# Where the output projection of a recurrent layer crosses from one block of instructions into the next: three tiles finished before the seam, one at once behind it

## The reference: what is computed

```
# layer 0, per head (8 heads of 128)
o = gla_chunked(q, k, v, log_f, s0, chunk)          # gated linear recurrence
o = rms_norm(o, norm_g) * silu(gate)
out = einsum('bte,ed->btd', o, w_out)               # 1152 x 1024 times 1024 x 1024
x = layer_norm(ALPHA * x + out, ln_g, ln_b)
# layer 1 starts with two projections of x
kv = einsum('btd,de->bte', x, w_dkv)
proj = einsum('btd,de->bte', x, w_in_b)             # 2560 columns
```

## Time and profile before

| | |
|---|---|
| median of 3 runs | 1989.67 us (1986.71 to 1990.49) |
| the profiled execution, own time | 1989.84 us |
| its span, first to last instruction | 1987.9 us |
| TensorE busy | 97% of the span, granted clock 0.989 in the mean |
| VectorE, ScalarE, GpSimd busy | 54%, 39%, 21% |
| last turn of block A, from the end of the last projection | 534.3 us |
| first matmul of block M | 579.3 us |
| first matmul behind the first two column tiles | 714.3 us |

### The profile page before, as it was taken

How to read it: one execution, slowest core, us unless ns; L and a number is a source line. 1 busy time by engine, 2 the same in 40 slices (tenths; PEclk the granted TensorE clock), 3 DMA queues, 4 the chain that set the end, 5 groups by cost and what they waited for, 6 DMA issues and landing times.

```text
span 1987.9 us, 31444 instructions
## 1 busy us (share of the span) xinstructions
PE 1927.6 (97%) x11755; PEld 1818.5 (91%) x11755; DVE 1071.4 (54%) x1941; ACT 768.5 (39%) x1343; POOL 408.2 (21%) x333
## 2 busy tenths in 40 slices
PE   8999999999969999999999999999999989999998
PEld 8999999999957899999989999999999979988886
DVE  4355545554747611332266666667666567753532
ACT  4333233323311131221265565555555457761100
POOL 0222132213322110000032432433433410000000
PEclk9999999999989999999999999999999999999999
DMA  5122022202344311224212112011111252363421
GB/s 173 40 75 67 21 66 76 65 22 67 114 148 141 102 46 57 75 78 129 89 38 66 34 53 64 28 50 47 53 47 41 68 135 68 94 243 133 153 85 43
DMA packets 189459, 158.82 MB, mean 80 GB/s; under 512 B 36192, under 2 KB 173920, under 8 KB 189120
## 3 DMA queue, kind: packets, MB, share of 16 engines
q1 hardware_dynamic: 183584, 137.31, 23.1%
q10 hardware_dynamic: 5328, 18.88, 2.6%
q0 software_dynamic: 464, 1.48, 0.2%
HBM read 115.78 MB, written 41.84 MB: 79 GB/s over the span
## 4 chain that ended last, share of the span: by engine, by line
PE 53%; DVE 8%; issue 5%; ACT 3%; DMA 1%; POOL 0%; DVEq 0%; ACTq 0%; SPq 0%; POOLq 0%
PE ps L115 16%; PE ps L117 16%; PE ps L116 15%; PE ps L1846 1%; PE ps L1829 1%; PE ps L1828 1%; DVE h_pt_l L109 1%; ACT h_p L1962 1%; ACT h_p L1951 1%; DVE h_p L2050 1%; DVE h_mx L2088 1%; DVE h_p L2045 1%; DVE s_mx L2689 1%; PE ps L2356 0%; DMA m_x<-in_x 0%
## 5 line engine op out<-in xcount | busy, mean ns | idle before, releaser
L1742 POOL TENSOR_SCALAR h_p<-h_p,h_rsum 128x128 f32<-128x128 f32 (+7 forms) x128 | 220.7, 1726 | 443.1 <-DVE h_rsum L2092 443.1
L115 PE MATMUL ps<-act_h,a_w_l 128*128 128x384 f32 x768 | 270.8, 353 | 1.7 <-DVE act_l L109 1.7
L117 PE MATMUL ps<-act_h,a_w_h 128*128 128x384 f32 x768 | 260.1, 339 | 0.0
L116 PE MATMUL ps<-act_l,a_w_h 128*128 128x384 f32 x768 | 259.9, 338 | 0.0
L115 PE MATMUL ps<-act_h,m_c_l 128*128 128x384 f32 x480 | 163.7, 341 | 4.2 <-DVE act_l L109 2.4
L116 PE MATMUL ps<-act_l,m_c_h 128*128 128x384 f32 x480 | 163.2, 340 | 0.0
L117 PE MATMUL ps<-act_h,m_c_h 128*128 128x384 f32 x480 | 163.1, 340 | 0.0
L115 PEld LDWEIGHTS ps<-act_h,a_w_l 128*128 128x128 f32 x768 | 144.2, 188 | 6.4 <-issue 3.3
L116 PEld LDWEIGHTS ps<-act_l,a_w_h 128*128 128x128 f32 x768 | 144.3, 188 | 3.3 <-issue 3.3
L117 PEld LDWEIGHTS ps<-act_h,a_w_h 128*128 128x128 f32 x768 | 144.1, 188 | 0.0
L104 ACT ACTIVATE h_pt_h<-ps 128x128 fp32r<-128x128 f32 (+2 forms) x192 | 87.0, 489 | 112.0 <-PE ps L1846 111.8
(11 more groups left out here) (321 smaller groups left out, 4863.5 us busy)
## 6 DMA issues: line engine op xcount, KB each, us to landing
a_w_raw<-in_w_in_a SPq DMA_DIRECT2D x32, 512.0 KB, 4.1
m_c_raw<-in_w_in_b SPq DMA_DIRECT2D x20, 512.0 KB, 4.2
scratch_gate<-m_sg SPq DMA_DIRECT2D x16, 576.0 KB, 5.2
o_w_raw<-in_w_out_b SPq DMA_DIRECT2D x16, 512.0 KB, 6.8
h_gate<-scratch_gate SPq DMA_DIRECT2D x62, 128.0 KB, 2.1
scratch_og<-h_gate SPq DMA_DIRECT2D x62, 128.0 KB, 1.7
o_g_raw<-scratch_og SPq DMA_DIRECT2D x24, 256.0 KB, 4.1
a_xn<-in_x SPq DMA_DIRECT2D x9, 512.0 KB, 4.3
```

The lines of the kernel that those rows point to most:

```text
L115: nc.tensor.matmul(out, ll, rh, start=first, stop=False)
L116: nc.tensor.matmul(out, lh, rl, start=False, stop=False)
L117: return nc.tensor.matmul(out, lh, rh, start=False, stop=last)
L1742: nc.gpsimd.tensor_scalar(weights_of(u), weights_of(u), rsum[:, u % PB], None, ALU.mult).then_inc(S["p_ready"], 1)
```

## The change

It redraws which part of the projection belongs to which block, and reorders the streams of block M to match.

* Block A: rows 0 to 7 of tiles 0, 1 and 2 (24 pairs). Row 6 of tiles 0 and 1 stands after step 15; all of tile 2 and row 7 of all three tiles stand behind the last step, `SOT`. The g buffers are now two pairs of tiles, (0,1) and (2,3), the second where `a_qq` to `a_kdec` were. Heads 0 to 6 of tiles 2 and 3 are loaded by one new transfer (896 KB). Row 7, the last head, is rounded straight from `a_sg`. `low_row(4)` and what follows it stand one place earlier on VectorE.
* Block M: TensorE starts with the product of tile 3, for which everything has been rounded in block A. Tile t is turned three products later than it is multiplied (two and two at the end) instead of one later. Its `sum_done` waits follow the new banks (`py`, `pt`).
* x(0) is the first transfer of SyncE's queue and x(1) the third; `load_x` serves tiles 2 to 8. The attention output comes in pairs of tiles. `kvw_raw` is loaded when the product of tile 7 is done (`y_done` 8), before when that of tile 2 was. `gain` and `shift` are the first transfers of GpSimd.
* `norm`: (x - mean) * gain and x * deviation + shift, each as two instructions of 512 columns on VectorE, in place of five instructions on VectorE and GpSimd.

```diff
 BESIDE_STEPS = {1: [(0, 1)], 3: [(0, 0)], 5: [(1, 1), (1, 0)], 7: [(2, 1), (2, 0)], 9: [(3, 1), (3, 0)],
-                11: [(4, 1), (4, 0)], 13: [(5, 1)], 15: [(5, 0)]}
+                11: [(4, 1), (4, 0)], 13: [(5, 1), (5, 0)], 15: [(6, 1), (6, 0)],
+                16: [(0, 2), (1, 2), (2, 2), (3, 2), (4, 2), (5, 2), (6, 2), (7, 0), (7, 1), (7, 2)]}
+
+OUT_PARTS = [(0, slice(0, EARLY), slice(0, 2)), (0, slice(EARLY, EARLY + 1), slice(0, 2)), (2, slice(0, EARLY + 1), slice(0, 1)),
+             (0, slice(KD - 1, KD), slice(0, 2)), (2, slice(KD - 1, KD), slice(0, 2)), (2, slice(0, EARLY + 1), slice(1, 2))]
...
+                    sp.wait_ge(operand[3], AH)
+                    sp.wait_ge(pe_did["SI"], AH)
+                    sp.wait_ge(pe_did["K1"], AH)
+                    sp.wait_ge(og_stored, 16 * (EARLY + 1))
+                    sp.dma_start(sh.g2_raw[:, 0:EARLY + 1].rearrange("p h a t -> p h (a t)"),
+                                 d["scratch_o"][0:EARLY + 1, :, 2 * P:4 * P].rearrange("h p t -> p h t")).then_inc(o_loaded[2], 16)
...
                     if not proj:
                         high_row(6)
+                        high_o(1)
+                        high_o(2)
                     copy_o("SO", 2, h)
                 if not proj:
                     high_row(7)
-                    high_o(1, slice(EARLY, EARLY + 1))
+                    high_o(3)
+                    high_o(4)
+                    high_o(5)
...
                     scores(1)
                     states(1)
+                    if not proj:
+                        low_row(4)
                     gated("OT0", 0)
...
+    def py(t):
+        b = (4, 0, 2, 6)[t] if t < 4 else (0, 2)[t % 2]
+        return bank[:, b:b + 2]
...
+        sp.dma_start(x[:, 0], row("x", 0)).then_inc(x_loaded[0], 16)
+        load_pair(4)
+        sp.dma_start(x[:, 1], row("x", 1)).then_inc(x_loaded[1], 16)
+        load_columns(0)
+        load_columns(1)
...
+        sp.wait_ge(y_done, 4)
+        load_pair(6)
+        sp.wait_ge(y_done, 5)
+        load_pair(8)
+        sp.wait_ge(y_done, 8)
+        sp.dma_start(kvw_raw[:], d["w_dkv"].rearrange("(a p) e -> p a e", p=P)).then_inc(kv_loaded, 16)
...
+        pe.sem_inc(y_done, 3)
+        for t in range(3, NT):
+            if t > 3:
+                pe.wait_ge(gl_ready, t - 3)
+                pe.wait_ge(sum_done, t - 2 if t < 6 else t - 1)
             for kt in range(nk):
...
+                last = rows_product(nc, py(t), sh, kt, t)
             last.then_inc(y_done, 1)
-            if t == 2:
-                turn_tile(0, 0, False)
-            turn_tile(t - 1, (t - 1) % 2, t >= 3)
+            if t < 7:
+                turn_tile(t - 3)
+            elif t == 7:
+                turn_tile(4)
+                turn_tile(5)
+            else:
+                turn_tile(6)
+                turn_tile(7)
...
+        pe.wait_ge(cl_ready, 2)
+        pe.wait_ge(sum_done, 8)
+        pe.wait_ge(tl_done, 4)
+        columns(1, 0)
+        pe.wait_ge(sum_done, 9)
+        columns(0, 0)
+        turn_tile(NT - 1)
+        pe.wait_ge(tl_done, 7)
+        columns(0, 1)
+        pe.wait_ge(tl_done, 9)
+        columns(1, 1)
...
+        for t in range(NT):
+            finish(t)
+            if t + 2 < NT:
+                load_x(t + 2)
+            if t < 3:
+                high_g(t + 6)
...
             for c in halves:
-                nc.vector.tensor_tensor(x[:, par, c], x[:, par, c], gain[:, c], ALU.mult).then_inc(gain_done, 1)
...
+                nc.vector.scalar_tensor_tensor(out=x[:, par, c], in0=x[:, par, c], scalar=mv[:, 0:1], in1=gain[:, c], op0=ALU.subtract, op1=ALU.mult).then_inc(gain_done, 1)
+
+            dve.wait_ge(rstd_step, t * 2 + 2)
+            for h, c in enumerate(halves):
+                dve.wait_ge(gain_done, t * 2 + 1 + h)
+                nc.vector.scalar_tensor_tensor(out=x[:, par, c], in0=x[:, par, c], scalar=rstd[:, 0:1], in1=shift[:, c], op0=ALU.mult, op1=ALU.add).then_inc(x_ready, 1)
```

More of the change, by code:

```diff
@@ L850, in body @@
                 if not proj:
-                    low_row(4)
+                    low_row(5)
                 if gla:
                     square(1)
+                    normed(1)
                     if not proj:
-                        low_row(5)
-                    normed(1)
+                        low_row(6)
+                        low_o(1)
                     sample_states(0)
@@ L860, in body @@
                     if not proj:
-                        low_row(6)
+                        low_o(2)
                     normed(2)
@@ L941, in middle_programs @@
     sh = k.shared
[L942 removed]
+    w_h, w_l = sh.w_h, sh.w_l
     cq_at = kept_at + 4 * 4 * T
@@ L1107, in _ @@
     def _(pool):
+        pool.dma_start(gain[:], ln_g.partition_broadcast(P)).then_inc(ln_loaded, 16)
+        pool.dma_start(shift[:], ln_b.partition_broadcast(P)).then_inc(ln_loaded, 16)
         nc.gpsimd.memset(mhalf[:], -0.5).then_inc(const_set, 1)
@@ L1191, in columns @@
                 mm.then_inc(c_done, 1)
-        for i in range(2):
-            pe.wait_ge(cl_ready, i + 1)
-            pe.wait_ge(sum_done, NT - 1 + i)
-            for tg in range(NTG - 1):
-                pe.wait_ge(tl_done, 4 + 3 * tg)
-                columns(i, tg)
-        turn_tile(NT - 1, (NT - 1) % 2, True)
+        pe.wait_ge(cl_ready, 2)
[9 more added lines that the diff above has]
+        columns(1, 1)
         pe.wait_ge(tl_done, NT + 1)
@@ L1402, in norm @@
             nc.vector.bn_aggr(mv[:], flat(stats[:])).then_inc(mv_done, 1)
-            dve.wait_ge(rstd_step, t * 2 + 2)
-            nc.vector.tensor_scalar(x[:, par], x[:, par], mv[:, 0:1], rstd[:, 0:1], ALU.subtract, ALU.mult).then_inc(norm_done, 1)
-            if isinstance(t, int) and t == 0:
+            if t == 0:
                 dve.wait_ge(ln_loaded, 32)
-            dve.wait_ge(norm_done, t + 1)
+            dve.wait_ge(mv_done, t + 1)
             halves = [slice(0, BANK), slice(BANK, D)]
             for c in halves:
-                nc.vector.tensor_tensor(x[:, par, c], x[:, par, c], gain[:, c], ALU.mult).then_inc(gain_done, 1)
-            dve.wait_ge(gain_done, t * 2 + 2)
-            nc.vector.tensor_tensor(x[:, par, halves[1]], x[:, par, halves[1]], shift[:, halves[1]], ALU.add).then_inc(x_ready, 1)
-        norm(0, 0)
-        norm(1, 1)
+                nc.vector.scalar_tensor_tensor(out=x[:, par, c], in0=x[:, par, c], scalar=mv[:, 0:1], in1=gain[:, c], op0=ALU.subtract, op1=ALU.mult).then_inc(gain_done, 1)
[3 more added lines that the diff above has]
+                nc.vector.scalar_tensor_tensor(out=x[:, par, c], in0=x[:, par, c], scalar=rstd[:, 0:1], in1=shift[:, c], op0=ALU.mult, op1=ALU.add).then_inc(x_ready, 1)
+        norm(0)
+        low_g(4)
+        norm(1)
+        turned_low(0)
+        low_g(5)
+        norm(2)
+        turned_low(1)
+        norm(3)
+        low_g(6)
         low_columns(0)
+        turned_low(2)
+        norm(4)
+        low_g(7)
         low_columns(1)
-        low_g(3)
-        turned_low(0, 0)
-        turned_low(1, 1)
-        for t in range(4, NT):
-            norm(t - 2, t % 2)
-            low_g(t)
-            turned_low(t - 2, t % 2)
-        norm(NT - 2, (NT - 2) % 2)
-        turned_low(NT - 2, (NT - 2) % 2)
-        norm(NT - 1, (NT - 1) % 2)
-        turned_low(NT - 1, (NT - 1) % 2)
+        turned_low(3)
+        norm(5)
+        low_g(8)
+        norm(6)
+        turned_low(4)
+        turned_low(5)
+        norm(7)
+        turned_low(6)
+        norm(8)
+        turned_low(7)
+        turned_low(8)
         dve.wait_ge(kvh_ready, 1)
```

176 lines of the change are left out of this document (76 added, 100 removed).

## The result

The changed kernel takes 2001.57 us in the median (1996.02 to 2002.21, five runs) against 1989.67 us before (1986.71 to 1991.50, five runs on the same chip); the ratio is 1.0051, 95% interval 1.0034 to 1.0069. That is slower by 7 to 14 us. The prediction was 1990.7 us with a range up to 1999, so the median lies 2.6 us above its end. The execution whose trace is read here took 1996.02 us; it is the fastest of the five. A second set of five executions on another chip gave 1997.29 against 1990.70 us, ratio 1.0037 [1.0023, 1.0051]; that median lies inside the range.

A forecast was written before the change was run, and what follows sets the result against it. TensorE, busy for 97% of the span, was taken to bound the kernel. Losses of 30.2 us afterwards against 29.3 before made it 0.9 us slower than the profiled 1989.84 us: 1990.7 us, range 1981 to 1999 us (8 in 10).

The forecast's parts named there:

- what block A loses: Block A up to `SOT`: the chain of VectorE and GpSimd to `SOT` was left 0.4 us of new loss.
- the clock behind the waits: Block M: TensorE at 1.2 GHz costs 0.8 us behind product 4's wait, 5.1 us behind those of products 6 to 8.
- Products 6, 7 and 8: Block M: each product waits for a sum whose x is loaded behind a turn; 5.9, 5.9 and 6.8 us, 18.6 together.
- `SOT` before 571: End of block A, a sign to look for in the profile after: `SOT` runs before 571 us, forecast at 569.7.
- The seam: Barrier from block A to block M: the last store's 7.46 us wait is covered, 1.9 us of idle stays.
- the seam gives nothing: Rival at the barrier: it takes 7.5 us whatever stands ahead, 5.6 us of gain fail, 1996 us; chance 0.04.
- Start of block M: Product 4 waits for norm(0), `low_g(4)` and norm(1)'s sum, starting at 14.3 instead of 11.8 us: 2.5 us lost.
- The rule of the Trainium skill on the clock: Waits for transfers always drop TensorE's clock: the three new waits would, block A's exit would cost none; sum unchanged.
- Lost before: Kernel before, 556 to 714 us: TensorE loses 20.4 us idle and 8.9 us by the clock, together 29.3 us.
- The end: End of block M: the 2.37 us wait goes; `columns(0, 0)` waits 0.9 us for norm(8)'s sum instead.
- Transfers collide at every wait: Rival on the x loads: landings of 6.5 us lengthen the waits by 9 us, 2000 us; chance 0.17.
- The three new waits are hidden: Rival at products 6 to 8: x arrives in time, 18.6 and 5.1 us are not lost, 1967 us; chance 0.10.

The follow-up runs named there:

- Three turns: Changed kernel with tiles 2, 3 and 4 transposed in the middle of products 5, 6 and 7 instead of behind them: 1980.03 us, ratio to before 0.9939.
- The stores of x: Changed kernel with finished x tiles stored by SyncE as soon as ready, not by ScalarE behind the next load: 1995.77 us, ratio to before 1.0032.
- Row 0: Changed kernel with row 0 of tile 0 waiting only for `g_out` and of tile 1 only for `v_out`: 1995.32 us, ratio to before 1.0026.
- The 1280 KB load: Changed kernel with `kvw_raw` loaded when the product of tile 8 is done, instead of tile 7: 2001.07 us, ratio to before 1.0056.

## Why the prediction was wrong

The three waits ahead of products 6 to 8 were there, as forecast in place and size. What failed are two terms of the sum: what block A loses, put at 0.4 us and measured 2.56, and the clock behind the waits, put at 5.9 us in all and measured 7.8. In the seam the sum came out too low by 4.3 us (185.25 less 180.03 less 0.9); against the other two traces of before it is 5.8 us. The median missed by 10.9 us (2001.57 against 1990.7), so the seam explains less than half of that; the rest stays open, as said at the end of this section. By its own steps:

* **Products 6, 7 and 8: right.** Forecast 5.9, 5.9 and 6.8 us, measured 5.92, 5.96 and 7.34: +0.6. *Three turns* shows the cause. Two errors inside nearly cancelled: the load is issued 0.9 us sooner than I took, and 512 KB land in 4.3 and 4.4 us, not 3.8, since a store runs beside them (*The stores of x*). That the size came out so close is in part luck. The landing of x(6), put at 5.5 us, took 6.6, beside 7.3 for `kvw_raw`, in the list of DMA issues by window:

```profile
m_x<-in_x ACTq DMA_DIRECT2D x1, 512.0 KB, 4.4
...
m_kvw_raw<-in_w_dkv SPq DMA_DIRECT2D x1, 1280.0 KB, 7.3
...
m_x<-in_x ACTq DMA_DIRECT2D x1, 512.0 KB, 6.6
```

* **What block A loses: the step that failed.** "I leave 0.4 us." It lost 2.56, because row 0 of tile 1 now stands behind `g_out`, which VectorE signals with the gating instruction `a_sg` (L845) at 538.21 + 1.34 us. I had followed the new banks of tile 2 and the steps around `SOT`, and passed over the two lines of the change that make row 0 of every tile wait for `g_out` and for `v_out`. *Row 0* shows the cause and the price. Without it `SOT` would have run some 2.6 us before its 573.64. The sign "`SOT` before 571" failed with it. Of the rest, the wait at row 4 went, and `SOT` came without idle. The 896 KB took 7.6 us (7 estimated); ScalarE waited 2.87 us for them, TensorE did not.
* **The seam: right.** 1.9 forecast, 1.60 measured; nothing of the last store's 7.46 us is left. The rival "the seam gives nothing" is refuted.
* **Start of block M: right.** 2.5 forecast, 0.71 + 1.26 = 1.97 measured in idle; product 4 starts 14.2 us behind the first matmul, 14.3 forecast, and VectorE got `shift` at 9.0 us, as taken. The clock behind it was put at 0.8; it was 1.5 in this trace and 0 in the second.
* **The clock behind the waits: the second step that failed, by its size.** Forecast 5.1, measured 1.4 + 2.0 + 2.9 = 6.3, and with the start of block M 7.8 against 5.9. The longest wait, 7.34 us, was followed by the longest stretch, 6.13 us; I had given all three the mean of two stretches of 4.0 and 4.8 us.
* **The rule of the Trainium skill on the clock.** The three long waits all dropped the clock, in both traces of the changed kernel, so with that section ("HAM oscillation", page "TensorE: Matmul & The Clock Gate") the trace agrees. It also agrees at the exit of block A, where the clock stayed at 1.00 behind 1.60 us. But the section warns only of longer gaps than 1.98 us, and behind those the clock fell in one trace of three, at a price of 1.6 us; there the measurement decides.
* **Lost before: over-counted.** The clock behind the wait at 558.62 was entered with its full stretch. Two of three traces don't have it, so the change had less to win than 29.3 us, by 1.6.
* **The end: right.** 0.9 forecast and 0.92 measured ahead of `columns(0, 0)`; the 2.37 us wait is gone.
* **"Transfers collide at every wait"** is refuted: x(4) and x(5) landed in 4.3 and 4.4 us. Only x(6) collided. **"The three new waits are hidden"** is refuted for this order, and the mechanism that hides them is the one it asked for, an earlier turn.

In the seam this makes +2.2 (block A) − 0.3 − 0.5 + 0.6 (waits) + 1.9 (clock) = 3.9 of the 4.3 us. The medians differ by 11.9 us in the first set and 6.6 in the second, the seams of the traces by 4.7 to 6.8 us over all pairs. So the second set agrees with the seam. In the first set the traced execution does too: it took 1996.02 us, 6.2 more than the traced one of before, with 5.2 of them in the seam. The median of that set lies 5.6 us above its own traced execution, and no trace of the changed kernel shows an execution as slow as that.

Where those 5.6 us lie is therefore not shown. Of the variants with the three long waits, two were traced at 2002 us. In *The stores of x* (2001.93 us, median 1995.77) the seam takes 185.80 us, but the part behind it 1277.8 us, against 1272.6 and 1274.8 in the changed kernel. In *The 1280 KB load* (2002.23 us) it is 187.60 us of seam and 1276.0 behind it. That speaks for some time lost behind the seam, where the variants don't differ; the three traces of before have 1273.3 to 1274.0 us there. Whether it is chance or an effect of the change was not settled.

## What to carry to other kernels

When a buffer is refilled by a load that waits for its last reader, count how much work stands in the bound engine's stream between that reader and the first user of the refill; if it is less than the chain of issue, landing and first use (here some 6 us), move the reader, not the transfer. Half a product between turn and use gave back 17 us here for a change of a few lines. And when a diff replaces one of two waits by both, price it at once, however far from the point of the change it stands.

## What the runs showed of the hardware that was not expected

* The granted clock after a short wait is not a function of its length. Behind 1.98 us of idle at the same instruction it fell to 0.51 once and stayed at 1.00 twice; behind the 1.26 us ahead of product 4 (with 0.71 and 1.09 us of idle one turn earlier) it fell to 0.56 in the first trace of the changed kernel and not in the second. Behind the long waits (5.7 us and more) of the changed kernel's two traces it fell each time.
* ScalarE issued a transfer 0.06 us behind the start of an instruction that takes 1.02 us, and not behind its end, where nothing else held the transfer up.
* 512 KB of x landed in 3.3 to 3.6 us alone, in 4.1 to 4.6 with a store of the same size issued behind them on the same queue, and in 6.5 to 7.1 beside a load of 1280 KB.
